# Hybrid decoder trunk: new places for row maxima, gate tiles, scan norm and latent tiles

## The chip, the cores and the metric

One core of a Trainium2 chip runs the whole two-layer trunk in one launch. The metric is device microseconds of that launch. The engines are told by short names: PE multiplies matrices, DVE and ACT do the elementwise work, SP issues the loads of weights, POOL issues the other transfers.

## The reference, cut to what matters

```python
D_MODEL, SEQ, DEPTH = 2048, 512, 2
def hybrid_layer(x, ...):
    h = rms_norm(x, norm_g)
    u = h @ w_in
    c_q, c_kv, k_pe, g_mla, u_conv, g_conv, z, xbc, dt_raw = jnp.split(u, offs, axis=-1)
    o_mla = mla_mixer(c_q, c_kv, k_pe, ...) * jax.nn.silu(g_mla)      # 6 heads, latent q 512, latent kv 256
    o_conv = conformer_conv_mixer(u_conv, ...) * jax.nn.silu(g_conv)  # 31 taps, 512 channels
    o_ssd = ssd_mixer(z, xbc, dt_raw, ...)                            # 12 heads, norm of y * silu(z)
    y = jnp.concatenate([o_mla, o_conv, o_ssd], axis=-1) @ w_out
    return x + y
```

`mla_mixer` norms c_q and c_kv, projects them, norms each head's query and key, rotates part of them and does causal softmax attention. `ssd_mixer` multiplies the scan's result y by silu(z) and norms it over its 768 channels.

## The kernel before, in words

All activations lie in SBUF with channels on partitions and the 512 positions along the free axis, 16 blocks of 128 channels. Every large product is done in three matmuls (L525 to L527): weights and activations are each split into a rounded part and the rest (`whi`, `wlo`; `hhi`, `hlo`), and the product of the two rests is left out.

**Units and tiles.** The input projection has 41 tiles of 128 output columns (`tiles_in`, L47): four cq, two ckv, one kpe, six gmla, eight of the convolution's input (ua and ug in turn), ten xbc, four gconv, six z. A tile is 16 blocks deep and is fed by two units of weights of 128x1024 (the first two tiles share four units, "first"). A unit takes PE 24 matmuls. For each, SP loads it into one of two `stage` buffers (L448), ACT copies it to one of three `whi` (L789) and DVE subtracts to make `wlo` (L1070). SP's load of a unit waits for the `wlo` of the unit two before. ACT's and DVE's share of unit u+3 is done at the beginning of step u, and ACT's waits until PE has used unit u.

**The order.** One list, `STEPS`, built by `steps` (L114) from the units and from `hooks` (L69), is walked by every engine. Step ("in", (j, half)) is half a tile, and the hooks at place 2j+half follow it. Each engine takes the list in order, so what waits on an engine holds back all that stands behind it there. On DVE a step first makes the `wlo` of unit u+3 and then, at half 1, takes the tile out of PSUM (`evac`, L1090). `acc_taken` counts those takings; PE waits for it before it begins a tile.

**Banks.** PSUM has eight banks: acc (2), S (2), T (2), M, O. Tiles alternate between the acc banks, but for tiles 2 and 3, which lie in S (`in_bank`, L314). Out rows use acc1, acc0, S0, T0 in turn.

**The latent tiles.** Hook "rx" (place 4) sums the squares of x on PE (`total`, L540: one fp32 matmul with ones into M); ACT turns it into 1/rms with an Ln and an Exp (`rsqrt`, L791, each with a table load). Then DVE and ACT run `latent` (L1186) for tiles 0 and 1 (evacuation, square, sum, split), and for tiles 2 to 5 at their own steps. Hook "cq_sum" (place 8) and "ckv_sum" (place 12) sum their squares on PE; for the latter ACT does Ln, Exp, Ln, Exp. Hooks "v" (places 13, 14) make the values in S and T, and ACT moves them out (L925). At the kpe tile ACT copies the rotated key half (`kr_both`), ahead of that.

**The attention.** For each of three pairs of heads: "proj", "head_sum" (sums of squares in S and T), ACT's Ln and Exp (`head_r`), "head_apply" for h=0 and h=1 (L1343: four DVE instructions each, the names `xg`, `key` for pair 2), "rotate". `row_max` and `row_rinv` (L1215) of score block n come at the beginning of step ("in", (14+n, 0)) on DVE; hook "scores" n is behind that step on PE and "turn_probs" n (transposes, L693) behind the next one.

**The end of a layer.** The scan's chunks (hooks "ssd_a", "ssd_b", places 54 to 72) write blocks 10 to 15 of `xg`; tile z i multiplies block 10+i by its gate and adds its square to `sqz` (three DVE instructions behind the gate, two for i=0). gconv i writes its gate to block 6+i, and "pw" f (places 78 to 81) multiplies the convolution's product into it. Step "turn" splits blocks 0 to 7 for the output projection. Step "ssd_sum" does the rest: blocks 8 and 9, ACT's Ln and Exp of the scan's sum (which PE makes in M within the second of the four "out2" units), then scaling and splitting of blocks 10 to 15. The out2 units hold output rows 0 and 1 in the order of `OUT2`:

```python
OUT2 = [(0, k) for k in range(10)] + [(1, k) for k in range(10)]
OUT2 += [(f, k) for f in range(2) for k in range(10, KX)]
```

## Time and profile before

| | |
|---|---|
| median of 3 runs | 1549.59 us (1548.27 to 1551.21) |
| the profiled execution | 1550.43 us |
| its span | 1548.6 us |
| PE busy | 1529.6 us, 99% |
| DVE busy | 1007.4 us, 65% |
| ACT busy | 687.2 us, 44% |
| mean granted clock | 0.999 |

A busy PE matmul of 512 columns is listed with 0.39 us, while back to back such matmuls start 0.23 us apart: the listed end of one overlaps the next. The stages of layer 0, by PE: start and first units to 37 us, latent tiles to 85, values to 110, projections to 216, attention beside tiles 14 to 26 to 430, scan beside the later tiles to 540, tail of the tiles to 601, output rows to 779. Layer 1 repeats them.

### The profile page before, as it was taken

To read this page: it belongs to the slowest core of one execution; us is meant where nothing else is said; L and a number is where in the kernel's file an instruction comes from. 1 tells how busy PE (TensorE), PEld (TensorE's weight loads), DVE (VectorE), ACT (ScalarE), POOL (GpSimd) and SP (SyncE) were. 2 spreads that over 40 slices of the span, in tenths; PEclk is the share of its full clock that TensorE was granted. 3 is DMA by queue.
4 is the path that set the end of the run, shared out by engine and by line. 5 is a ranking of instruction groups with operands and counts; after the bars stand their busy time and mean duration, and the time that the engine had idled before them with its cause. 6 is when DMAs were issued, how large, how long until landed. Compare 5 with 4: busy or idle time off the path is not lost.

```text
span 1548.6 us, 18424 instructions
## 1 busy us (share of the span) xinstructions
PE 1529.6 (99%) x7086; PEld 1225.9 (79%) x7086; DVE 1007.4 (65%) x1497; ACT 687.2 (44%) x1015; POOL 43.6 (3%) x84
## 2 busy tenths in 40 slices
PE   9999999999999999999999999999999999999999
PEld 7777777778888787788887777778778888878887
DVE  7544674989998777443455456658899978673221
ACT  7455543434456645211153555533444565552111
POOL 0000000000000000110000000000000000001010
PEclk9999999999999999999999999999999999999999
DMA  6322222222233223544432222222223333235442
GB/s 226 98 89 82 86 86 75 71 80 68 82 110 116 88 83 99 165 139 154 143 107 78 82 87 91 82 69 82 69 69 103 97 118 105 69 95 170 143 149 82
DMA packets 44839, 158.13 MB, mean 102 GB/s; under 512 B 5552, under 2 KB 5840, under 8 KB 44752
## 3 DMA queue, kind: packets, MB, share of 16 engines
q1 hardware_dynamic: 38448, 134.36, 26.8%
q0 software_dynamic: 6304, 22.60, 5.2%
q8 instruction: 56, 0.92, 0.2%
q14 instruction: 31, 0.25, 0.0%
HBM read 148.50 MB, written 8.44 MB: 101 GB/s over the span
## 4 chain that ended last, share of the span: by engine, by line
PE 82%; DVE 10%; ACT 5%; issue 2%; DMA 1%; SPq 0%; DVEq 0%; ACTq 0%
PE acc L525 18%; PE acc L527 18%; PE acc L526 18%; PE S L530 5%; PE S L525 3%; PE S L527 3%; PE S L526 3%; PE T L527 3%; PE T L526 3%; PE T L525 3%; DVE wlo L1070 2%; ACT L777 1%; PE M L530 1%; PE O L530 1%; DVE hlo L1173 1%
## 5 line engine op out<-in xcount | busy, mean ns | idle before, releaser
L525 PE MATMUL acc<-hhi,whi 128*128 128x512 f32 (+1 forms) x1504 | 599.9, 399 | 6.4 <-DVE wlo L1070 3.2
L527 PE MATMUL acc<-hhi,wlo 128*128 128x512 f32 (+1 forms) x1504 | 587.1, 390 | 0.0
L526 PE MATMUL acc<-hlo,whi 128*128 128x512 f32 (+1 forms) x1504 | 586.5, 390 | 0.0
L1070 DVE TENSOR_TENSOR wlo<-stage,whi 128x1024 fp32r<-128x1024 f32 (+2 forms) x251 | 299.5, 1196 | 409.2 <-ACT whi L789 405.8
L789 ACT ACTIVATE whi<-stage 128x1024 fp32r<-128x1024 f32 (+2 forms) x251 | 259.1, 1036 | 501.8 <-PE acc L527 282.8
L525 PEld LDWEIGHTS acc<-hhi,whi 128*128 128x128 f32 (+1 forms) x1504 | 281.5, 187 | 72.9 <-DVE wlo L1070 4.9
L527 PEld LDWEIGHTS acc<-hhi,wlo 128*128 128x128 f32 (+1 forms) x1504 | 281.3, 187 | 61.9
L526 PEld LDWEIGHTS acc<-hlo,whi 128*128 128x128 f32 (+1 forms) x1504 | 281.7, 187 | 60.3 <-issue 2.9
L1125 DVE SCALAR_TENSOR_TENSOR cacc<-glu,pv,cacc 128x512 f32<-128x512 f32 x240 | 168.8, 747 | 4.0
L777 ACT ACT_TABLE_LOAD x67 | 86.0, 1283 | 3.0 <-DVE small L1061 1.1
L525 PE MATMUL S<-hhi,whi 128*128 128x512 f32 x192 | 75.2, 392 | 0.1
L526 PE MATMUL S<-hlo,whi 128*128 128x512 f32 x192 | 74.7, 389 | 0.0
L527 PE MATMUL S<-hhi,wlo 128*128 128x512 f32 x192 | 74.7, 389 | 0.0
L525 PE MATMUL T<-hhi,whi 128*128 128x512 f32 x128 | 49.8, 389 | 0.0
L526 PE MATMUL T<-hlo,whi 128*128 128x512 f32 x128 | 49.8, 389 | 0.0
L527 PE MATMUL T<-hhi,wlo 128*128 128x512 f32 x128 | 49.8, 389 | 0.0
L1061 DVE SCALAR_TENSOR_TENSOR xb<-raw,pv,xb 128x512 f32<-128x512 f32 x60 | 45.0, 751 | 2.4
L777 ACT ACTIVATE prob<-S,cols 128x128 f32<-128x128 f32 (+3 forms) x48 | 25.4, 529 | 44.8 <-DVE cols L1222 38.4
L525 PEld LDWEIGHTS S<-hhi,whi 128*128 128x128 f32 x192 | 36.0, 188 | 8.6 <-DVE wlo L1070 1.0
L526 PEld LDWEIGHTS S<-hlo,whi 128*128 128x128 f32 x192 | 36.0, 188 | 7.7 <-issue 0.2
L527 PEld LDWEIGHTS S<-hhi,wlo 128*128 128x128 f32 x192 | 36.0, 188 | 7.5
L891 ACT ACTIVATE xb<-raw,pv 128x512 f32<-128x512 f32 x20 | 16.4, 819 | 46.5 <-DVE raw L1052 46.5
(239 smaller groups left out, 1566.2 us busy)
## 6 DMA issues: line engine op xcount, KB each, us to landing
stage<-weights SPq DMA_DIRECT2D x235, 512.0 KB, 3.4
y_features<-xg POOLq DMA_DIRECT2D x30, 256.0 KB, 4.2
acsb<-acs_rows POOLq DMA_DIRECT2D x16, 384.0 KB, 4.1
xr<-x_features POOLq DMA_DIRECT2D x16, 256.0 KB, 4.1
xr<-y_features POOLq DMA_DIRECT2D x16, 256.0 KB, 4.0
...
```

The lines of the kernel that those rows point to most:

```text
L525: nc.tensor.matmul(out, a, c, start=start, stop=False)
L526: nc.tensor.matmul(out, a, d, start=False, stop=False)
L527: return nc.tensor.matmul(out, b, c, start=False, stop=stop)
L530: return nc.tensor.matmul(out, a, b, start=start, stop=stop)
L777: nc.scalar.activation(out, in_, func, **more).then_inc(signal.sem, 1)
L789: nc.scalar.activation(whi[u % RING][:, 0:w], stage[u % STAGE][:, 0:w], ACT.Copy).then_inc(hi_done.sem, 1)
L891: nc.scalar.activation(xb[i // 5][:, i % 5, :], raw[:, 3:3 + SEQ], ACT.Identity, scale=par("scw", SSD_K * ch + 3), bias=par("scb", ch)).th ...
L1061: d(signal, nc.vector.scalar_tensor_tensor(out=out, in0=x, scalar=s, in1=y, op0=op0, op1=op1), go)
L1070: nc.vector.tensor_tensor(wlo[u % RING][:, 0:w], stage[u % STAGE][:, 0:w], whi[u % RING][:, 0:w].bitcast(F32), ALU.subtract).then_inc(lo_d ...
L1125: ins = nc.vector.scalar_tensor_tensor(out=cacc[:, j, :], in0=src, scalar=wt, in1=cacc[:, j, :], op0=ALU.mult, op1=ALU.add)
L1173: nc.vector.tensor_tensor(hlo[:, k, :], xg[:, k, :], hhi[:, k, :].bitcast(F32), ALU.subtract).then_inc(h_lo.sem, 1)
```

## The change

1. Tiles 0 to 5 use six banks (acc, S, T). PE's waits follow: tiles 6 and 7 wait for tiles 0 and 1, in layer 1 tiles 2 and 4 wait for the last output rows. "rx" goes from place 4 to 6 and then takes latent tiles 0 to 2; "cq_sum" goes from 8 to 10.
2. ACT's four operations at "ckv_sum" become Ln, Ln, Exp, Exp; its copy for `kr_both` goes from the kpe tile to "kd_turn".
3. The last pair's `head_apply` does both queries and the first key at once; `row_max(0)`, the second key and `row_rinv(0)` come at the beginning of step ("in", (13, 1)), ahead of that step's weights.
4. Tile order at the end: z0 to z2, gconv0, gconv1, z3 to z5, gconv2, gconv3.
5. The scan's sum is made on PE at place 79 (in T1) and its scaling on DVE at place 80, both ahead of the last tile. Step "turn_end" then splits blocks 10 to 15, 8, 9, and the output rows 0 and 1 take the blocks in that order.

```diff
-    t += [("gconv", j, [(_OFF["gconv"] + P * j, P)]) for j in range(4)]
-    t += [("z", j, [(_OFF["z"] + P * j, P)]) for j in range(6)]
-    return t
+    return t + z[0:3] + gate[0:2] + z[3:6] + gate[2:4]
...
-    put(4, "rx")
-    put(8, "cq_sum")
+    put(6, "rx")
+    put(10, "cq_sum")
...
+    put(79, "ssd_sum")
+    put(80, "ssd_scale")
...
+TURN_ORDER = list(range(8)) + list(range(10, KX)) + [8, 9]
+OUT2 = [(f, k) for f in range(2) for k in TURN_ORDER[:8]]
+OUT2 += [(f, k) for f in range(2) for k in TURN_ORDER[8:14]]
+OUT2 += [(f, k) for f in range(2) for k in TURN_ORDER[14:]]
...
-            return S[j - 2] if j in (2, 3) else acc[j % 2]
+            return (acc + S + T)[j] if j < 6 else acc[j % 2]
...
-                        if half == 0 and j >= 4:
-                            pe.wait_ge(acc_taken.sem, acc_taken.at(layer, j - 1))
+                        if half == 0 and j >= 6:
+                            pe.wait_ge(acc_taken.sem, acc_taken.at(layer, j - 5 if j < 8 else j - 1))
...
+                    elif name == "ssd_sum":
+                        pe.wait_ge(ssd_sq.sem, ssd_sq.at(layer, 1))
+                        pe.wait_ge(ssd_in.sem, ssd_in.at(layer, 8))
+                        total(ssd_sum, [sqz[:, :]], T[1])
                     elif name == "out2":
                         quarter, u = args[0], own[0]
                         if quarter < 2:
                             pe.wait_ge(acc_taken.sem, acc_taken.at(layer, len(TILES) - 1 + quarter))
-                        if quarter == 1:
-                            pe.wait_ge(ssd_sq.sem, ssd_sq.at(layer, 1))
-                            pe.wait_ge(pw_taken.sem, pw_taken.at(layer, 4))
-                            total(ssd_sum, [sqz[:, :]], M)
...
-                        rsqrt(None, rkc, O[:, 0:4], KV_LORA, 0)
-                        rsqrt(lat_r, rckv[:, :], M[:, :], KV_LORA, 0)
+                        a(None, rkc, O[:, 0:4], ACT.Ln, scale=1.0 / KV_LORA, bias=eps_col[:, 0:1])
+                        a(None, rckv[:, :], M[:, :], ACT.Ln, scale=1.0 / KV_LORA, bias=eps_col[:, 0:1])
+                        a(None, rkc, rkc, ACT.Exp, scale=-0.5)
+                        a(lat_r, rckv[:, :], rckv[:, :], ACT.Exp, scale=-0.5)
                     elif name == "kd_turn":
+                        act.wait_ge(kr_half.sem, kr_half.at(layer, 1))
+                        a(kr_both, kr2[64:128, :], kr2[0:64, :], ACT.Copy)
...
                 for name, args, own in STEPS:
-                    row_step = args[0] - SCORES_FROM if name == "in" and args[1] == 0 else -1
-                    if 0 <= row_step < 12:
+                    if name == "in" and args == (SCORES_FROM - 1, 1):
+                        row_max(0)
+                        apply_key(2, 1)
+                        row_rinv(0)
+                    row_step = args[0] - SCORES_FROM if name == "in" and args[1] == 0 else 0
+                    if 0 < row_step < 12:
                         row_max(row_step)
                     for u in own:
                         split(u + RING)
...
-                    elif name == "ssd_sum":
-                        split_branch(8, 10)
+                        split_branch(TURN_ORDER[:8], 0)
+                    elif name == "ssd_scale":
                         dve.wait_ge(ssd_r.sem, ssd_r.at(layer, 1))
                         for k in range(10, KX):
                             stt(branch_ready, xg[:, k, :], xg[:, k, :], par("sng", k - 10), rcq[:, :], ALU.mult,
                                 ALU.mult, go=k < KX - 1)
-                            if k >= 12:
-                                split_branch(k - 2, k - 1)
-                        split_branch(KX - 2, KX)
+                    elif name == "turn_end":
+                        split_branch(TURN_ORDER[8:], 8)
```

DVE at the first score block, before (`S` and `cols` are the row maxima's, `xg` and `key` the last pair's heads, `wlo` the weights' rests):

```order
L1070 TENSOR_TENSOR wlo_60<-stage_53,whi_57 128x1024
L1292 MEMSET glu 128x30
L1061 SCALAR_TENSOR_TENSOR glu<-acc,rx 128x512
L1061 SCALAR_TENSOR_TENSOR xg<-xg,pv,sqh 128x512
L1061 SCALAR_TENSOR_TENSOR xg<-xg,pv,sqh 64x512
L1061 SCALAR_TENSOR_TENSOR key_80<-key_80,pv,sqh 128x512
L1052 TENSOR_TENSOR key_80<-kr_91,sqh 64x512
L1052 TENSOR_TENSOR S<-S,const 128x128
L1222 TENSOR_REDUCE cols<-S 128x1
L1052 TENSOR_TENSOR S<-S,const 128x128
L1222 TENSOR_REDUCE cols<-S 128x1
L1070 TENSOR_TENSOR wlo_58<-stage_54,whi_55 128x1024
```

and with the change:

```order
L1067 SCALAR_TENSOR_TENSOR xg<-xg,pv,sqh 128x512
L1067 SCALAR_TENSOR_TENSOR xg<-xg,pv,sqh 64x512
L1067 SCALAR_TENSOR_TENSOR key_80<-key_80,pv,sqh 128x512
L1058 TENSOR_TENSOR key_80<-kr_91,sqh 64x512
L1058 TENSOR_TENSOR S<-S,const 128x128
L1228 TENSOR_REDUCE cols<-S 128x1
L1058 TENSOR_TENSOR S<-S,const 128x128
L1228 TENSOR_REDUCE cols<-S 128x1
L1067 SCALAR_TENSOR_TENSOR key_80<-key_80,pv,sqh 128x512
L1058 TENSOR_TENSOR key_80<-kr_91,sqh 64x512
L1235 RECIPROCAL cols<-cols 128x1 x2
L1076 TENSOR_TENSOR wlo_60<-stage_53,whi_57 128x1024
```

The two masked maxima stand ahead of the second key, and the weights' rest and the evacuation of tile 13 (`glu<-acc`) behind all of it.

ACT between the latent sums and the values, before (`cols` and `rckv` are the roots, `kr` the key half):

```order
L777 ACT_TABLE_LOAD
L777 ACTIVATE cols<-O,eps_col 128x4
L777 ACT_TABLE_LOAD
L777 ACTIVATE cols<-cols 128x4
L777 ACT_TABLE_LOAD
L777 ACTIVATE rckv<-M,eps_col 128x512
L777 ACT_TABLE_LOAD
L777 ACTIVATE rckv<-rckv 128x512
L789 ACTIVATE whi_56<-stage_53 128x768
L777 ACTIVATE kr_91<-kr_91 64x512
L789 ACTIVATE whi_57<-stage_54 128x1024
L925 ACTIVATE value<-S,cols 128x384 x2
```

and with the change:

```order
L781 ACT_TABLE_LOAD
L781 ACTIVATE cols<-O,eps_col 128x4
L781 ACTIVATE rckv<-M,eps_col 128x512
L781 ACT_TABLE_LOAD
L781 ACTIVATE cols<-cols 128x4
L781 ACTIVATE rckv<-rckv 128x512
L793 ACTIVATE whi_56<-stage_53 128x768
L793 ACTIVATE whi_57<-stage_54 128x1024
L930 ACTIVATE value<-S,cols 128x384 x2
L930 ACTIVATE value<-T,cols 128x384 x2
```

Two table loads are gone, and the copy of the key half no longer stands ahead of the values.

DVE from the turn on, before (after the eight splits of blocks 0 to 7):

```order
L1070 TENSOR_TENSOR wlo_59<-stage_53,whi_56 128x1024
L1052 TENSOR_TENSOR xg<-O,xg 128x512
L1070 TENSOR_TENSOR wlo_60<-stage_54,whi_57 128x1024
L1052 TENSOR_TENSOR temp<-acc,rx 128x512
L1052 TENSOR_TENSOR xg<-xg,temp_69 128x512
L1052 TENSOR_TENSOR temp<-xg 128x512
L1052 TENSOR_TENSOR kr_91<-kr_91,temp 128x512
L1070 TENSOR_TENSOR wlo_58<-stage_53,whi_55 128x1024
L1052 TENSOR_TENSOR xg<-M,xg 128x512
L1173 TENSOR_TENSOR hlo<-xg,hhi 128x512 x2
L1061 SCALAR_TENSOR_TENSOR xg<-xg,pv,rcq 128x512 x3
```

and with the change, from those eight splits on:

```order
L1179 TENSOR_TENSOR hlo<-xg,hhi 128x512 x8
L1076 TENSOR_TENSOR wlo_59<-stage_53,whi_56 128x1024
L1058 TENSOR_TENSOR xg<-O,xg 128x512
L1067 SCALAR_TENSOR_TENSOR xg<-xg,pv,rcq 128x512 x6
L1076 TENSOR_TENSOR wlo_60<-stage_54,whi_57 128x1024
L1058 TENSOR_TENSOR temp<-acc,rx 128x512
L1076 TENSOR_TENSOR wlo_58<-stage_53,whi_55 128x1024
L1058 TENSOR_TENSOR xg<-M,xg 128x512
L1179 TENSOR_TENSOR hlo<-xg,hhi 128x512 x8
```

The six scalings by `rcq` stand ahead of the last tile's evacuation (`temp<-acc`), and all eight remaining splits follow in one piece.

## Rows read from the trace of the kernel before

**Rows 1.** PE's waits over the whole span: engine, line, releaser, us in total, times, longest us.

```profile
PE acc L525 <- DVE wlo L1070: 3.2, 4, 1.4
PE T L693 <- ACT prob L777: 3.2, 2, 1.6
PE S L525 <- ACT value L925: 2.3, 2, 1.1
```

**Rows 2.** Timeline of PE: start us, us, engine line, out<-in, shape, count, [idle before <-releaser].

```profile
38.66 0.50 PE L525 MATMUL S<-hhi,whi 128*128 128x512 f32 x1
...
60.33 0.39 PE L527 MATMUL acc<-hhi,wlo 128*128 128x512 f32 x1
62.15 1.10 PE L530 MATMUL M<-sqh,ones 128*128 128x512 f32 x2 [1.43 <-DVE sqh L1052]
```

**Rows 3.** Timeline of DVE at the sum of squares' end in layer 0.

```profile
37.38 2.36 DVE L1070 TENSOR_TENSOR wlo<-stage,whi 128x1024 fp32r<-128x1024 f32 x2
```

**Rows 4.** Timeline of PE in layer 1 at the sum of the input's squares.

```profile
806.61 1.02 PE L530 MATMUL M<-sqh,ones 128*128 128x512 f32 x2
...
807.70 0.40 PE L526 MATMUL S<-hlo,whi 128*128 128x512 f32 x1
```

**Rows 5.** Timeline of ACT in layer 1 behind that sum.

```profile
807.94 1.28 ACT L777 ACT_TABLE_LOAD   x1
```

**Rows 6.** Timeline of DVE in layer 1, the first two latent tiles and a weight unit.

```profile
811.96 0.69 DVE L1052 TENSOR_TENSOR temp<-acc,rx 128x512 f32<-128x512 f32 x1 [2.78 <-ACT rx L777]
...
814.36 0.69 DVE L1052 TENSOR_TENSOR temp<-acc,rx 128x512 f32<-128x512 f32 x1
...
817.32 1.23 DVE L1070 TENSOR_TENSOR wlo<-stage,whi 128x1024 fp32r<-128x1024 f32 x1
```

**Rows 7.** Timeline of ACT ahead of the value rows.

```profile
100.73 0.63 ACT L777 ACTIVATE kr<-kr 64x512 f32<-64x512 f32 x1 [6.60 <-DVE kr L1052]
```

**Rows 8.** Timeline of PE around the first transposed probabilities, layer 0.

```profile
237.20 0.76 PE L693 MATMUL T<-const,prob 128*128 128x128 f32 x2 [1.59 <-ACT prob L777]
237.73 0.47 PE L525 MATMUL acc<-hhi,whi 128*128 128x512 f32 x1
...
240.16 0.63 PE L526 MATMUL acc<-hlo,whi 128*128 128x512 f32 x1
240.59 0.63 PE L527 MATMUL acc<-hhi,wlo 128*128 128x512 f32 x1
```

**Rows 9.** Stretch: us, PE busy (count), PEld, DVE, ACT, POOL, PEclk, DMA share, GB/s.

```profile
236.00:242.00 6.00, 4.69 (x14) 3.61 (x15) 3.29 (x6) 2.94 (x6) 0.00 (x0) 0.72 0.41 109
```

**Rows 10.** Timeline of DVE before those transposes.

```profile
226.23 1.40 DVE L1061 SCALAR_TENSOR_TENSOR xg<-xg,pv,sqh 128x512 f32<-128x512 f32 x2 [3.66 <-ACT sqh L777]
...
234.03 0.30 DVE L1052 TENSOR_TENSOR S<-S,const 128x128 f32<-128x128 f32 x1
```

**Rows 11.** Timeline of DVE at the weights behind a gate tile.

```profile
497.47 1.23 DVE L1070 TENSOR_TENSOR wlo<-stage,whi 128x1024 fp32r<-128x1024 f32 x1 [2.23 <-ACT whi L789]
```

**Rows 12.** Timeline of PE at the end of the tiles and in the first output rows.

```profile
593.15 0.40 PE L525 MATMUL acc<-hhi,whi 128*128 128x512 f32 x1
...
598.62 0.40 PE L525 MATMUL M<-pwhi,whi 128*128 128x512 f32 x1
...
607.42 1.10 PE L530 MATMUL M<-kr,ones 128*128 128x512 f32 x2 [0.35 <-DVE xg L1052]
608.85 0.50 PE L525 MATMUL acc<-hhi,whi 128*128 128x512 f32 x1 [0.33 <-DVE hlo L1173]
...
621.49 0.50 PE L525 MATMUL acc<-hhi,whi 128*128 128x512 f32 x1 [1.37 <-DVE wlo L1070]
```

**Rows 13.** Timeline of DVE from the turn to the scan's scaling.

```profile
594.01 4.90 DVE L1173 TENSOR_TENSOR hlo<-xg,hhi 128x512 fp32r<-128x512 f32 x8 [1.98 <-ACT hhi L807]
...
599.97 0.68 DVE L1052 TENSOR_TENSOR xg<-O,xg 128x512 f32<-128x512 f32 x1
...
612.50 2.08 DVE L1061 SCALAR_TENSOR_TENSOR xg<-xg,pv,rcq 128x512 f32<-128x512 f32 x3 [3.10 <-ACT rcq L777]
```

More of the change, by code:

```diff
@@ L57, in tiles_in @@
             t += [("xbc", 5 * g + i, [(_OFF["xbc"] + P * c, P)])]
-    t += [("gconv", j, [(_OFF["gconv"] + P * j, P)]) for j in range(4)]
-    t += [("z", j, [(_OFF["z"] + P * j, P)]) for j in range(6)]
-    return t
+    gate = [("gconv", j, [(_OFF["gconv"] + P * j, P)]) for j in range(4)]
+    z = [("z", j, [(_OFF["z"] + P * j, P)]) for j in range(6)]
+    return t + z[0:3] + gate[0:2] + z[3:6] + gate[2:4]
 TILES = tiles_in()
@@ L144, in steps @@
     return s, units
-OUT2 = [(0, k) for k in range(10)] + [(1, k) for k in range(10)]
-OUT2 += [(f, k) for f in range(2) for k in range(10, KX)]
+TURN_ORDER = list(range(8)) + list(range(10, KX)) + [8, 9]
+OUT2 = [(f, k) for f in range(2) for k in TURN_ORDER[:8]]
+OUT2 += [(f, k) for f in range(2) for k in TURN_ORDER[8:14]]
+OUT2 += [(f, k) for f in range(2) for k in TURN_ORDER[14:]]
 STEPS, UNITS = steps()
@@ L568, in _ @@
                         u, m = own[0], tile_columns(j)
-                        if half == 0 and j >= 4:
-                            pe.wait_ge(acc_taken.sem, acc_taken.at(layer, j - 1))
-                        if half == 0 and j == 2 and layer:
-                            pe.wait_ge(acc_taken.sem, acc_taken.at(layer - 1, len(TILES) + KX - 1))
+                        if half == 0 and j >= 6:
+                            pe.wait_ge(acc_taken.sem, acc_taken.at(layer, j - 5 if j < 8 else j - 1))
+                        if half == 0 and j in (2, 4) and layer:
+                            pe.wait_ge(acc_taken.sem, acc_taken.at(layer - 1, len(TILES) + KX - 2 + j // 2))
                         for k8 in range(8):
@@ L874, in _ @@
                         kind, i, _ = TILES[args[0]]
-                        if kind in ("cq", "ckv") and args[0] >= 2:
+                        if kind in ("cq", "ckv") and args[0] >= 3:
                             latent_hi(args[0])
-                        if kind == "kpe":
-                            act.wait_ge(kr_half.sem, kr_half.at(layer, 1))
-                            a(kr_both, kr2[64:128, :], kr2[0:64, :], ACT.Copy)
                         if kind == "ug":
@@ L898, in _ @@
                         rsqrt(rx_ready, rx[:, :], M[:, :], D_MODEL, 0)
-                        for j in range(2):
+                        for j in range(3):
                             latent_hi(j)
@@ L1015, in _ @@
                     elif name == "ssd_sum":
+                        act.wait_ge(ssd_sum.sem, ssd_sum.at(layer, 1))
+                        rsqrt(ssd_r, rcq[:, :], T[1][:, :], SSD_WIDTH, 0)
+                    elif name == "turn_end":
                         act.wait_ge(unit_used.sem, unit_used.at(layer, TILE_UNIT[len(TILES) - 1] + 1))
-                        act.wait_ge(pw_taken.sem, pw_taken.at(layer, 4))
-                        for k in range(8, KX):
-                            if k == 10:
-                                act.wait_ge(ssd_sum.sem, ssd_sum.at(layer, 1))
-                                rsqrt(ssd_r, rcq[:, :], M[:, :], SSD_WIDTH, 0)
+                        for k in TURN_ORDER[8:]:
                             if k >= 10:
                                 act.wait_ge(branch_ready.sem, branch_ready.at(layer, k - 9))
+                            else:
+                                act.wait_ge(pw_taken.sem, pw_taken.at(layer, k - 5))
                             branch_hi(k)
@@ L1167, in _, with split_branch @@
                                 x_add(3 * (k // 8) + i)
-                def split_branch(first, end):
-                    for k in range(first, end):
-                        dve.wait_ge(h_hi.sem, h_hi.at(layer, KX + k + 1))
+                def split_branch(ks, before):
+                    for i, k in enumerate(ks):
+                        dve.wait_ge(h_hi.sem, h_hi.at(layer, KX + before + i + 1))
                         nc.vector.tensor_tensor(hlo[:, k, :], xg[:, k, :], hhi[:, k, :].bitcast(F32),
@@ L1229, in row_rinv, with apply_query, apply_key @@
                         d(rinv_ready, nc.vector.reciprocal(rinv[h], rsum[h]))
[L1231 to L1233 removed]
+                def apply_query(p, h):
+                    q, r = QK[p], slice(64 * h, 64 * h + 64)
+                    stt(None, q[h], q[h], par("qn"), sqh[:, h, :], ALU.mult, ALU.mult, go=True)
+                    stt(None, q[2][r], q[2][r], par("qr")[r], sqh[r, h, :], ALU.mult, ALU.mult)
+                def apply_key(p, h):
+                    q, r = QK[p], slice(64 * h, 64 * h + 64)
+                    stt(None, q[3 + h], q[3 + h], par("kn"), sqh[:, 2 + h, :], ALU.mult, ALU.mult, go=True)
+                    tt(None, q[5][r], kr2[r, :], sqh[r, 2 + h, :], ALU.mult)
+                for name, args, own in STEPS:
+                    if name == "in" and args == (SCORES_FROM - 1, 1):
[4 more added lines that the diff above has]
+                    if 0 < row_step < 12:
                         row_max(row_step)
@@ L1260, in _ @@
                         kind, i, _ = TILES[j]
-                        if kind in ("cq", "ckv"):
+                        if kind in ("cq", "ckv") and j >= 3:
                             latent(j)
@@ L1464, in _ @@
                     elif name == "rx":
-                        for j in range(2):
+                        for j in range(3):
                             latent(j)
                     elif name == "turn":
-                        split_branch(0, 8)
-                    elif name == "ssd_sum":
-                        split_branch(8, 10)
+                        split_branch(TURN_ORDER[:8], 0)
+                    elif name == "ssd_scale":
                         dve.wait_ge(ssd_r.sem, ssd_r.at(layer, 1))
```

22 lines of the change are left out of this document (12 added, 10 removed).

## The prediction

> **What bounds the kernel now.** PE is listed busy for 99% of the span, and the change takes no matmul away and adds none, so only the time can go in which PE stands still. I first read PE's waits over the whole span [rows 1]: a handful, in the same places in both layers. Then PE's timeline at each of them gives its size. A unit of 24 matmuls takes 598.62 - 593.15 = 5.47 us, 0.23 us a matmul [rows 12], while a row lists 0.39; so a stall is the idle time shown plus 0.16. Check: the matmul at 60.33 should be followed at 60.56, the next work begins at 62.15, 1.59 late, and 1.43 + 0.16 is the same [rows 2]. So per layer: values 2.3 / 2 + 0.16, about 1.3 [rows 1]; first transposes 1.59 + 0.16 = 1.75 [rows 8]; output rows 0.35, 0.33 and 1.37, each + 0.16, together 2.53 [rows 12]. Layer 0 alone has the 1.59 at the cq sum. One thing more: behind the stall at 237.20 matmuls start 240.59 - 240.16 = 0.43 us apart and not 0.23 [rows 8]: the granted clock fell to 1.2 GHz of 2.4 after 1.75 us of standing still. Its mean over 236 to 242 is 0.72 [rows 9], which makes 0.28 x 6 = 1.7 us of work not done. The same stall in layer 1 did not bring that: the mean clock of the whole execution is 0.999, which is this one stretch (1.7 / 1548.6).
>
> **The sum, part by part.**
>
> *Six banks, later latent tiles.* The sum of the input's squares costs PE 807.70 - 806.61 - 0.23 = 0.86 us [rows 4]. In layer 0 it costs nothing now: PE may go on with tile 2 only at 38.66, since the unit's `wlo` ends at about 38.6, behind DVE's adding of squares [rows 2, 3]. Moved two units on, it leaves that wait uncovered and is paid in full: +0.86. In return the cq sum comes two units later. Its wait of 1.59 goes if all is in time. Take PE's begin of the square sum as zero. ACT finishes a `whi` at +1.3 and the roots at +5.3 (807.94 and 811.96 less 806.61) [rows 4 to 6]. The first latent tile takes 814.36 - 811.96 = 2.40, each further one 817.32 - 814.36 = 2.96, so three end at +13.7 and the `wlo` behind them at +14.9 [rows 6]. PE needs it after the sum and three units, at 0.86 + 3 x 5.47 = +17.3: 2.4 us to spare. Tile 3 is squared 2.1 us after that `wlo` (the 2.96 less its split of 0.8), at +17, and the cq sum needs it at +22.7. Tiles 4 and 5 no longer wait for a bank. So nothing else is late: 0.86 - 1.59 = -0.73, layer 0 only.
>
> Here a rule has to be weighed. A table load is listed with 1.28, and from the first load's start to the end of both roots there are 4.0 us (two loads, 0.7 and 0.6) [rows 5, 6]: nothing is added to a load. The Trainium skill ("ScalarE: Activation LUTs", What ACT_TABLE_LOAD costs) says that every switch of set costs about 2.66 us, load and drain together. By that, the roots would come at +8.1 and the `wlo` at +17.7, 0.4 late in each layer, and the sum below would be 0.8 smaller. The rows decide: I take 1.28.
>
> *Values.* The second value unit waits for ACT's first values, and those stand behind the copy of the key half, for which ACT idles 6.60 us until 100.73 [rows 7]. The copy moves behind the values, to where its 0.63 us stands between a gate and the dt chain, which PE meets two units later. Two loads fewer (2.6 us) start the rest earlier. First value tiles can then leave some 4 us earlier than now, against a stall of 1.3: all of it goes, in both layers. The first matmul after a stall also takes longer to the next, 0.1 us; with the stalls below four per layer, I take -0.2 a layer for that.
>
> *First row maxima.* DVE begins the last pair's heads at 226.23 and the maxima at 234.03, 7.8 us later [rows 10]. In between lie two heads of four instructions of 0.7 (two take 1.40), a `wlo` of 1.2 and an evacuation of 0.7. With the change six of the eight head instructions come first: 226.23 + 4.3 = 230.5. PE's scores are there one unit before its 235.45 (below), at 230.0. Four instructions of 0.3 end at 231.8, the second key at 233.2, the reciprocals at 233.6, ACT's scaling of the first head at 234.0, and PE is free at 237.20 - 1.75 = 235.45. Margin 1.4 us, so 1.75 goes, and so does what the second head's transposes wait between themselves: the two take 237.73 - 237.20 = 0.53 now and should take 0.22 [rows 8]. -2.06 in each layer. Behind the maxima on DVE's queue stand the `wlo` of PE's next unit (ready at 234.8, needed at 235.7) and the evacuation of tile 13, done at 235.6, which PE needs only after its transposes at 235.7. That one is near, and I leave it at nothing. With the stall the slow stretch should go, 1.7 us, once.
>
> *z tiles ahead.* Each brings two or three DVE instructions of 0.7, at most 2.15 us, before the next `wlo`. At those places DVE idles 2.23 and more in front of that `wlo`, waiting for ACT and so for PE [rows 11]. Cost nothing. Without that cover it would be up to 2.15 a tile, but the weights are three units ahead, and only a delay of more than a unit would reach PE.
>
> *The scan's norm ahead of the turn.* PE's sum costs the same 0.86 in its new place. There it follows z5's tile by two units and two pointwise products of 12 matmuls (2.8 each), some 16 us, so its input is ready. Behind it PE has a unit and the third product, 8.2 us, until the turn; ACT needs about 1.3 for a `whi`, as above, and 4.0 for the roots, and has them 3 us before the turn. Now the turn itself; zero is the end of that product, 593.3, some 0.86 later in the new order. The eight splits end at +5.6, the `wlo` and the product's gate at +7.4 (599.97 + 0.68) [rows 13]. Six scalings at 2.08 / 3 = 0.69 end at +11.5, the next `wlo` at +12.7, the evacuation of tile 40 at +13.3. PE needs the latter for output row 1, after a unit, the last product (2.8) and the first out2 unit: 2 x 5.47 + 2.8 - 0.16 = +13.6. Margin 0.3 us, the tightest of the change. From there: gate, `wlo` and product to +17, eight splits at 0.6 to +21.9, the first of them at +17.7 for a need at +19.0, and each next one needed 0.68 later. The next `wlo` comes at +23.1 for +24.5. So all three stalls go: -2.53 a layer. If splits and scalings had stayed behind the sum, as now, nothing would. The last two of the four waits for `wlo` in rows 1, (3.2 - 2 x 1.37) / 2 = 0.23 each, stand behind the first pointwise product, and they stay: nothing ahead of them changes.
>
> Sum: layer 0: -0.73 - 1.3 - 2.06 - 1.7 - 2.53 - 0.2 = -8.5; layer 1: -1.3 - 2.06 - 2.53 - 0.2 = -6.1; together -14.6. From the profiled execution's 1550.43: **1535.8 us**. That execution is 0.84 above the median of the runs shown, which may well be its one stretch of half clock; runs without it would go from some 1548.8 to the same 1535.8.
>
> **The rivals.** *B, the half clock comes all the same.* PE still stands still for 1.1 us at 37.5 and at the start; one such stretch costs 1.7: 1537.5. For it: it came once in two equal stalls. Against: no other stall brought it.
>
> *C, a cover fails in part.* The margins of 0.3 us (tile 40's evacuation) and 0.1 (tile 13's) are no larger than what two equal stretches differ by, and three latent tiles in a row are a new burst. Should the maxima still be late by what they are now, 4.1 come back and perhaps the 1.7: 1541.6; half of it, 1538.8.
>
> *D, the stalls only move.* Each time PE comes sooner, it waits as long at the next thing. Then only the slow stretch goes, 1550.43 - 1.7 = 1548.7. Against: every chain that I followed starts from PE's own progress (a bank done, a unit used), so it moves with PE.
>
> *E, slower: the turn's chain stands bare.* DVE now does six scalings (4.1), the last `wlo` (1.2) and the evacuation (0.7) between the pointwise product and output row 1, and they wait for ACT's 4.0 us of roots. If those roots came only after the turn's splits, all 10 us would stand before PE in each layer: 1535.8 + 20 = 1556. It decides where DVE reaches the scaling more than 7 us later than reckoned; then the change loses. Against: the roots are reckoned 3 us ahead of the turn and over 10 us ahead of the scaling.
>
> **How the numbers follow.** As reckoned (1535.0 to 1537.0): 0.60. B: 0.14. C: 0.14. More goes than reckoned (another 0.4 to 0.8 of small waits; under 1534.6): 0.05. D: 0.04. E: 0.03. The forecast is the first. The range runs from 1534.4 to 1540.5, over B and most of C, and leaves out D, E and C's far end. About 0.2%, 3.1 us, is what a measurement of this kernel can tell from no change: faster 0.93 (all but D and E), same 0.04, slower 0.03.
>
> **What would show it.** In the changed kernel's waits of PE: no wait for `prob` at L693's new line, none for `value`, none ahead of the sum over `kr`, and none of 1.4 for `wlo` in the out rows; 0.23 for the pointwise product still there; a wait of about 1 us for `wlo` at 37.5. The clock at 2.4 GHz from the start to the end. DVE's evacuation of tile 40 ends just before PE's first matmul of output row 1. It would be wrong if a new wait on `acc` evacuation or `wlo` of over 0.5 us appears, at tile 13, behind the three latent tiles, or in output row 1.

## The result and the profile after

The changed kernel takes 1534.78 us in the median (1534.68 to 1534.90, 4 runs) beside 1549.07 us (1548.27 to 1551.21, 4 runs) for the kernel before: a ratio of 0.9905, with a 95% interval of 0.9893 to 0.9917. The profiled execution took 1534.9 us with a span of 1533.1, against 1550.43 and 1548.6: 15.5 us less. The forecast was 1535.8, with a range from 1534.4 to 1540.5: the measured time lies inside it, and 0.2 below the case that was given 0.60 (1535.0 to 1537.0).

The page of the changed kernel, from its parts on busy time and on the chain:

```profile
span 1533.1 us, 18419 instructions
...
PE 1524.4 (99%) x7086; PEld 1225.4 (80%) x7086; DVE 1007.6 (66%) x1497; ACT 683.0 (45%) x1013; POOL 43.5 (3%) x84
...
PE 92%; DVE 5%; ACT 1%; issue 1%; DMA 0%; SPq 0%; DVEq 0%; ACTq 0%
```

The same work is done; ACT is busy for 4.2 us less, with 65 table loads and not 67. Each layer saves two loads at the ckv sum and has one more behind the scan's roots, which now stand amid the gate tiles (loads at 580.69, 582.69 and 594.30, where the kernel before has two, at 608.53 and 610.54). The waits of PE in the changed kernel, over the whole span, answer to [rows 1]:

```profile
PE acc L529 <- DVE wlo L1161: 1.1, 1, 1.1
PE M L534 <- DVE eps_col L1038: 1.1, 1, 1.1
PE acc L529 <- DVE hlo L1144: 1.1, 2, 0.8
PE S L529 <- DVE wlo L1076: 1.0, 1, 1.0
PE acc L529 <- DVE wlo L1076: 0.4, 2, 0.2
PE S L534 <- DVE sqh L1058: 0.3, 1, 0.3
```

The waits for `prob` (3.2) and `value` (2.3) are gone, and so are the two of 1.4 for `wlo` in the output rows. L1161, L1144 and `eps_col` belong to the start. What is left is the uncovered 1.0 that the forecast had for layer 0, 0.2 a layer behind the first pointwise product, and one wait of 0.3 that the kernel before has too (945.22 there). PE's timeline shows the uncovered wait at its place, against [rows 2], and then the sum of squares (an fp32 matmul is listed as two):

```profile
37.63 0.50 PE L529 MATMUL S<-hhi,whi 128*128 128x512 f32 x1 [1.03 <-DVE wlo L1076]
...
48.64 1.02 PE L534 MATMUL M<-sqh,ones 128*128 128x512 f32 x2
```

DVE of the changed kernel around the first row maxima, which answers to [rows 10]:

```profile
226.09 0.75 DVE L1067 SCALAR_TENSOR_TENSOR key<-key,pv,sqh 128x512 f32<-128x512 f32 x1
226.76 0.68 DVE L1058 TENSOR_TENSOR key<-kr,sqh 64x512 f32<-64x512 f32 x1
227.47 0.30 DVE L1058 TENSOR_TENSOR S<-S,const 128x128 f32<-128x128 f32 x1
...
230.29 0.36 DVE L1235 RECIPROCAL cols<-cols 128x1 f32<-128x1 f32 x2
230.69 1.22 DVE L1076 TENSOR_TENSOR wlo<-stage,whi 128x1024 fp32r<-128x1024 f32 x1
231.87 0.08 DVE L1314 MEMSET glu<- 128x30 f32 x1
231.98 0.69 DVE L1067 SCALAR_TENSOR_TENSOR glu<-acc,rx 128x512 f32<-128x512 f32 x1
```

and PE behind it, against [rows 8]:

```profile
232.31 0.38 PE L697 MATMUL T<-const,prob 128*128 128x128 f32 x2
232.82 0.47 PE L529 MATMUL acc<-hhi,whi 128*128 128x512 f32 x1
```

Both transposes run without a wait, but the next tile starts at 232.82, 0.15 behind the end of tile 13's evacuation (231.98 + 0.69 = 232.67). That start is 0.29 later than 232.31 + 0.22 = 232.53, where PE would have been free: a new small wait. The windows of 8 us from 234 on, before and after (us, then busy times by engine, then PEclk, the granted clock), against [rows 9]:

```profile
234.00:242.00 8.00, 6.30 (x22) 4.59 (x21) 5.12 (x10) 3.86 (x10) 0.00 (x0) 0.79 0.30 82
```

```profile
234.00:242.00 8.00, 8.00 (x39) 6.23 (x39) 4.26 (x8) 3.88 (x8) 0.00 (x0) 1.00 0.53 168
```

The clock stays at 2.4 GHz. At the turn, DVE of the changed kernel, against [rows 13]:

```profile
588.35 4.91 DVE L1179 TENSOR_TENSOR hlo<-xg,hhi 128x512 fp32r<-128x512 f32 x8 [1.96 <-ACT hhi L811]
593.17 1.22 DVE L1076 TENSOR_TENSOR wlo<-stage,whi 128x1024 fp32r<-128x1024 f32 x1
594.30 0.69 DVE L1058 TENSOR_TENSOR xg<-O,xg 128x512 f32<-128x512 f32 x1
595.02 4.07 DVE L1067 SCALAR_TENSOR_TENSOR xg<-xg,pv,rcq 128x512 f32<-128x512 f32 x6
599.12 1.23 DVE L1076 TENSOR_TENSOR wlo<-stage,whi 128x1024 fp32r<-128x1024 f32 x1
600.27 0.68 DVE L1058 TENSOR_TENSOR temp<-acc,rx 128x512 f32<-128x512 f32 x1
```

and PE's first matmul of output row 1:

```profile
601.24 0.39 PE L529 MATMUL acc<-hhi,whi 128*128 128x512 f32 x1
```

The evacuation of tile 40 ends at 600.95, 0.29 ahead of PE; the forecast said 0.3.

**Where the 15.5 us came from.** PE's starts of the same matmuls in both traces (for the last matmul, its end), and how much more the changed kernel is ahead at each:

| up to | before | after | ahead by | of it here |
|---|---|---|---|---|
| third group of the first unit (start) | 11.95 | 10.91 | 1.04 | 1.04 |
| ckv sum of layer 0 | 84.89 | 83.13 | 1.76 | 0.72 |
| transposes of `kd` | 112.80 | 109.67 | 3.13 | 1.37 |
| first product of probabilities and values | 246.48 | 239.95 | 6.53 | 3.40 |
| last product `pw` | 598.62 | 592.96 | 5.66 | -0.87 |
| ckv sum of layer 1 | 851.98 | 842.45 | 9.53 | 3.87 |
| transposes of `kd` | 879.88 | 868.99 | 10.89 | 1.36 |
| first product of probabilities and values | 1012.28 | 999.69 | 12.59 | 1.70 |
| last `pw` | 1364.42 | 1352.69 | 11.73 | -0.86 |
| end of the last matmul | 1545.35 | 1529.77 | 15.58 | 3.85 |

The 0.86 is the scan's sum, now ahead of `pw` 3 and no longer in the output rows; the turn is worth 3.0 net in each layer. A full 1.0 us lies in the first 12 us, where nothing was changed:

```profile
11.95 0.50 PE L525 MATMUL acc<-hhi,whi 128*128 128x512 f32 x1 [1.76 <-DVE hlo L1138]
```

```profile
10.91 0.50 PE L529 MATMUL acc<-hhi,whi 128*128 128x512 f32 x1 [0.81 <-DVE hlo L1144]
```

Ahead of the first of these ACT had waited 1.75 us for a load of weights and began the second `whi` at 9.11; in the changed kernel it began it at 8.13, 0.98 earlier.

### The profile page after: what moved, and what is told of

Read it like the earlier page. It is cut to its first block, busy times and chain, and to the rows that moved or that the text cites. A ratio compares the mean times of both kernels' runs of the same rounds, so it can differ in the third digit from the quotient of the medians.

```text
span 1533.1 us, 18419 instructions
## 1 busy us (share of the span) xinstructions
PE 1524.4 (99%) x7086; PEld 1225.4 (80%) x7086; DVE 1007.6 (66%) x1497; ACT 683.0 (45%) x1013; POOL 43.5 (3%) x84
## 4 chain that ended last, share of the span: by engine, by line
PE 92%; DVE 5%; ACT 1%; issue 1%; DMA 0%; SPq 0%; DVEq 0%; ACTq 0%
PE acc L529 20%; PE acc L531 19%; PE acc L530 19%; PE S L534 5%; PE S L529 4%; PE S L530 4%; PE S L531 4%; PE T L531 4%; PE T L530 4%; PE T L529 4%; PE M L534 1%; PE O L534 1%; DVE wlo L1076 1%; PE T L534 1%; PE T L697 1%
## 5 line engine op out<-in xcount | busy, mean ns | idle before, releaser
L529 PE MATMUL acc<-hhi,whi 128*128 128x512 f32 (+1 forms) x1440 | 573.8, 398 | 2.9 <-DVE wlo L1161 1.1
L531 PE MATMUL acc<-hhi,wlo 128*128 128x512 f32 (+1 forms) x1440 | 561.7, 390 | 0.0
L530 PE MATMUL acc<-hlo,whi 128*128 128x512 f32 (+1 forms) x1440 | 560.8, 389 | 0.0
L531 PEld LDWEIGHTS acc<-hhi,wlo 128*128 128x128 f32 (+1 forms) x1440 | 268.9, 187 | 59.3
L529 PE MATMUL T<-hhi,whi 128*128 128x512 f32 x192 | 75.5, 393 | 0.0
L531 PE MATMUL T<-hhi,wlo 128*128 128x512 f32 x192 | 74.7, 389 | 0.0
L530 PE MATMUL T<-hlo,whi 128*128 128x512 f32 x192 | 74.7, 389 | 0.0
L529 PEld LDWEIGHTS T<-hhi,whi 128*128 128x128 f32 x192 | 36.0, 188 | 7.9 <-issue 0.5
L530 PEld LDWEIGHTS T<-hlo,whi 128*128 128x128 f32 x192 | 36.0, 188 | 7.9 <-issue 0.5
L531 PEld LDWEIGHTS T<-hhi,wlo 128*128 128x128 f32 x192 | 36.0, 188 | 7.5
```

Source lines behind the costliest of these rows:

```text
L529: nc.tensor.matmul(out, a, c, start=start, stop=False)
L530: nc.tensor.matmul(out, a, d, start=False, stop=False)
L531: return nc.tensor.matmul(out, b, c, start=False, stop=stop)
```

## Experiments

The theory is the forecast's: each stall stands alone, so each part can be undone alone and gives back its own term. The main rival: the parts cover one another. Five kernels undo one part of the change or half of one, and two do one part alone. Where not said otherwise five or four runs were timed.

### The row maxima back

```diff
-                    if name == "in" and args == (SCORES_FROM - 1, 1):
-                        row_max(0)
-                        apply_key(2, 1)
-                        row_rinv(0)
-                    row_step = args[0] - SCORES_FROM if name == "in" and args[1] == 0 else 0
+                    row_step = args[0] - SCORES_FROM if name == "in" and args[1] == 0 else -1
...
```

with `head_apply` for h=0 and h=1 as before.

> The changed kernel (1534.8) with the order of the last pair's heads and of the first row maxima as before. Theory, every stall stands alone: PE waits for the first probabilities again, 1.75 us in each layer, and the small wait of 0.3 behind tile 13's evacuation is covered by it, so about +3.5 us: 1538.3, clock 2.4 GHz throughout or, if the long stall brings the half clock, up to 1540.0 with a stretch of 1.2 GHz right behind it in layer 0. Rival, the parts cover one another (the earlier values already bring the scores forward): under +1, 1535.8 at most.

Measured: 1540.1 us (1538.09 to 1540.46, 5 runs). Its waits hold the old one again, and the window from 234 on, beside the same stretch of layer 1 (997 to 1003), shows the clock:

```profile
PE T L697 <- ACT prob L781: 3.4, 2, 1.7
```

```profile
234.00:240.00 6.00, 5.50 (x17) 4.29 (x18) 2.56 (x4) 2.88 (x6) 0.00 (x0) 0.72 0.54 168
...
997.00:1003.00 6.00, 5.31 (x24) 4.26 (x24) 2.72 (x5) 2.94 (x6) 0.00 (x0) 1.00 0.50 169
```

PE stands still for 1.86 us ahead of 234.40 and for 1.88 ahead of 997.59 (1.70 and 1.72 idle + 0.16). Behind the first the clock falls, with a mean of 0.72 as in [rows 9]; behind the second it doesn't. Four of the five runs lie at 1540.1 to 1540.5, with a mean granted clock of 0.999 on record; the one at 1538.09 has 1.000. So the stalls alone give the 1538.3 of the theory, and a stretch of half clock on top of them the 1540. The rival (under 1536) is out.

### The scan's norm back at the turn

```diff
-    put(79, "ssd_sum")
-    put(80, "ssd_scale")
...
+                        if quarter == 1:
+                            pe.wait_ge(ssd_sq.sem, ssd_sq.at(layer, 1))
+                            pe.wait_ge(pw_taken.sem, pw_taken.at(layer, 4))
+                            total(ssd_sum, [sqz[:, :]], M)
```

with the old `OUT2`, scaling and splits; the tile order stays new.

> The changed kernel with the scan's sum, roots, scaling and the order of the splits at the turn as before; the order of the last ten tiles stays new. Theory: the three stalls of output rows come back (0.51, 0.50 and 1.54 of standing still, and a slow second matmul behind each), +3.0 us a layer, 1540.8. Rival, the new tile order already puts the sum's squares earlier and takes part of the waits: 1536 to 1538.

Measured: 1539.32 us (1539.16 to 1539.79), 2.2 a layer and not 3.0. PE's timeline around the sum:

```profile
600.31 0.39 PE L527 MATMUL acc<-hhi,wlo 128*128 128x512 f32 x1
600.54 1.09 PE L530 MATMUL M<-kr,ones 128*128 128x512 f32 x2
601.96 0.50 PE L525 MATMUL acc<-hhi,whi 128*128 128x512 f32 x1 [0.33 <-DVE hlo L1174]
```

The sum starts 0.23 behind the matmul ahead of it: the first of the three stalls of [rows 12] isn't there. In layer 1 most of the second is gone too: the next matmul starts 1.10 behind the sum's start (1362.74 and 1363.84), against 1.42 above. The time lies between the theory's 1540.8 and the rival's 1538, and the rival is right in part: the new tile order took these waits, as the next run shows.

### The tile order alone

The kernel before with the new `tiles_in` and nothing else.

> The kernel before with the new order of the last ten tiles and nothing else. Theory, DVE's two or three more instructions behind a z tile stand in its idle time: no difference from the kernel before (ratio 1.000). Rival, a wlo comes late behind them: up to +2 us a layer. Rival, the earlier squares shorten the waits of the output rows: -1 to -2 us.

Measured: 1546.53 us (1545.74 to 1548.49, 11 runs), ratio 0.9983 (0.9974 to 0.9992). The last rival holds. In DVE's timeline the gate of the last pointwise product ends before PE's sum, which starts at 605.82, has to wait:

```profile
603.64 1.23 DVE L1070 TENSOR_TENSOR wlo<-stage,whi 128x1024 fp32r<-128x1024 f32 x1 [2.22 <-ACT whi L789]
604.79 0.69 DVE L1052 TENSOR_TENSOR xg<-M,xg 128x512 f32<-128x512 f32 x1
```

In the kernel before the three instructions of z5 (2.15 us) stood ahead of that `wlo`, which started at 605.45, and the gate ended at 607.27. With gconv3 last they are not there. The wait of 0.33 behind the sum is smaller as well, 0.21 in layer 0. Between the last `pw` and the ckv sum of the next layer the trace is 0.69 shorter (851.98 - 598.62 = 253.36 before, 850.20 - 597.53 = 252.67 here), and from the last `pw` of layer 1 to the end 0.78: 1.5 in all. The medians differ by 2.65 (1549.18 for the kernel before); 13 of its 19 runs have a mean clock under 1.000, against 4 of 11 here. Compared at the same recorded clock they differ by 1.8 (1547.90 and 1546.11 at 1.000, six and seven runs) and by 1.3 (1549.27 and 1547.93 at 0.999).

### The values: the copy, or the loads

```diff
                         if kind == "kpe":
+                            act.wait_ge(kr_half.sem, kr_half.at(layer, 1))
+                            a(kr_both, kr2[64:128, :], kr2[0:64, :], ACT.Copy)
```

> The changed kernel with ACT's copy of the rotated key at the kpe tile again, ahead of the values; the roots stay in the order Ln, Ln, Exp, Exp. Theory, the copy was what the values stood behind: the second value unit waits about 1.3 us in each layer again, +2.7: 1537.5. Rival, the two saved table loads did it: 0 to +0.3, 1535.1 at most.

and, the other way round, the copy late and the roots apart:

```diff
-                        a(None, rkc, O[:, 0:4], ACT.Ln, scale=1.0 / KV_LORA, bias=eps_col[:, 0:1])
...
+                        rsqrt(None, rkc, O[:, 0:4], KV_LORA, 0)
+                        rsqrt(lat_r, rckv[:, :], M[:, :], KV_LORA, 0)
```

> The changed kernel with the roots of the ckv sum in the order Ln, Exp, Ln, Exp (two table loads more in each layer, 2.6 us of ACT); the key's copy stays late. Theory, the copy was the cause and the loads only cost time that ACT has: 0, 1534.8. Rival, the loads were the cause: +1 to +2.7, up to 1537.5.

Measured: 1535.71 us (1535.5 to 1535.85) with the copy back, 1535.14 (1535.04 to 1535.3) with the roots apart. ACT's and PE's timelines of the kernel with the copy back:

```profile
97.88 0.63 ACT L781 ACTIVATE kr<-kr 64x512 f32<-64x512 f32 x1 [6.60 <-DVE kr L1059]
98.54 1.06 ACT L793 ACTIVATE whi<-stage 128x1024 fp32r<-128x1024 f32 x1
99.51 1.03 ACT L931 ACTIVATE value<-S,cols 128x384 f32<-128x384 f32 x2
```

```profile
100.21 0.41 PE L529 MATMUL S<-whi,ckvhi 128*128 128x384 f32 x1 [0.26 <-ACT value L931]
```

The values still stand behind the copy, as in [rows 7], but counted from the ckv sum (82.91 here, 84.89 before) the copy comes at +15.0 and not at +15.8. The loads cost ACT 2.6 us, of which 0.9 reaches DVE's work on the key, since ACT then idles for 1.72 until PE frees the buffer of its next `whi`. So the stall shrinks to 0.26 + 0.16 = 0.42, twice 0.42 = 0.84 in all, and 1535.71 is 0.8 to 0.9 above the changed kernel (1534.91 in the runs below, 1534.78 above). That is neither the theory's 1537.5 nor the rival's 1535.1 at most: each had one cause do all. With the roots apart there is no wait for `value`, and the first value leaves 12.63 us behind the ckv sum, the same as in the changed kernel (83.27 and 83.13 are the sums):

```profile
95.90 1.03 ACT L928 ACTIVATE value<-S,cols 128x384 f32<-128x384 f32 x2
```

```profile
95.76 1.03 ACT L930 ACTIVATE value<-S,cols 128x384 f32<-128x384 f32 x2
```

Moving the copy takes the whole stall of 1.3; the two loads saved, with the copy in its old place, take 0.9 of it. They are not additive.

### The latent tiles back

```diff
-    put(6, "rx")
-    put(10, "cq_sum")
+    put(4, "rx")
+    put(8, "cq_sum")
...
-            return (acc + S + T)[j] if j < 6 else acc[j % 2]
+            return S[j - 2] if j in (2, 3) else acc[j % 2]
```

> The changed kernel with two banks for tiles 0 and 1 and S for 2 and 3, and the sums of squares at places 4 and 8 again. Theory: the wait of 1.59 at the cq sum of layer 0 returns and the wait of 1.0 for the third unit's rest hides behind the sum again; net +0.7, layer 0 only: 1535.5. Rival, the six banks also save in layer 1: +1.5 or more. Rival, they save nothing: 0.

> The same kernel as e3_latents_back, whose profiled execution was disturbed (4889 us). Theory: in layer 0 the cq sum waits 1.6 us again and the 1.0 at the third unit's rest goes, and layer 1 stays: a span 0.7 us longer than the changed kernel's, 1535.5. The timed runs of e3_latents_back (1535.6 to 1536.1) say that it may be 1.2; then the trace should show a second wait.

Measured: 1535.64 to 1536.09 us in three timed runs (the profiled execution, at 4891 us, is left out), and the second time 1535.57 us (1534.81 to 1535.67), beside the changed kernel run again:

> The changed kernel, unaltered, beside the three others: 1534.8, within 0.3 us.

Measured for the unaltered kernel: 1534.91 us (1534.73 to 1535.12). So +0.7, or up to 1.1 by the first. The second trace puts it at 0.93: from the third group of matmuls to the ckv sum it takes 83.80 - 10.65 = 73.15, the changed kernel 83.13 - 10.91 = 72.22, and behind that both take the same. That trace has the wait that the theory names, and no other that the changed kernel lacks:

```profile
PE M L534 <- DVE sqh L1058: 1.6, 1, 1.6
```

Behind it PE had stood still for 1.57 + 0.16 = 1.73 us, and the clock of the next 6 us is 2.4 GHz all the same:

```profile
61.00:67.00 6.00, 5.98 (x25) 4.62 (x26) 1.89 (x2) 4.29 (x5) 0.00 (x0) 1.00 0.24 73
```

### The maxima alone

The kernel before with the maxima's part of the change.

> The kernel before with the last pair's heads and the first row maxima moved and nothing else. Theory: 1.75 us less in each layer, and no stretch of half clock: against runs of the kernel before without such a stretch -3.5 us, against runs with it -5.2. Rival, without the earlier values and the rest the maxima are not earlier against PE: under 1 us.

Measured: 1544.36 us (nine runs from 1544.04 to 1544.96, one at 1548.35), ratio 0.9975 (0.9965 to 0.9984); the median is 4.8 less than that of the runs of before beside it (1549.18, 19 runs). Both numbers of the theory can be read off at the recorded clocks: against the six of these runs with a mean clock of 1.000 (median 1547.90) the nine runs gain 3.6, against those with 0.999 (1549.27) 5.0. In the trace the clock is 1.0, and it gains 3.37 us in layer 0 and 1.74 in layer 1 at this place (214.47 and 246.48 against 213.47 and 242.11; 981.88 and 1012.28 against 977.50 and 1006.16), as with the whole change. This part needs none of the others.

### How near tile 40's evacuation is

```diff
+                        tt(None, temp[:, :], rcq[:, :], rcq[:, :], ALU.mult)
+                        tt(None, temp[:, :], rcq[:, :], rcq[:, :], ALU.mult)
                     elif name == "turn_end":
```

> The changed kernel with two further DVE instructions of 0.7 us right behind the six scalings of the scan's blocks (their result is not used). It measures how near the evacuation of tile 40 is to output row 1. Theory: PE has 0.3 us to spare there, so 1.4 - 0.3 = 1.1 us appear as a wait ahead of output row 1 in each layer: +2.2, with the slow matmul behind a stall +2.4: 1537.2. Rival, the evacuation is not what binds and its time can be made up: 0.

Measured: 1537.07 us (1536.92 to 1537.26). DVE and PE:

```profile
599.11 1.42 DVE L1058 TENSOR_TENSOR temp<-rcq 128x512 f32<-128x512 f32 x2
600.57 1.23 DVE L1076 TENSOR_TENSOR wlo<-stage,whi 128x1024 fp32r<-128x1024 f32 x1
601.71 0.68 DVE L1058 TENSOR_TENSOR temp<-acc,rx 128x512 f32<-128x512 f32 x1
```

```profile
602.49 0.47 PE L529 MATMUL acc<-hhi,whi 128*128 128x512 f32 x1 [1.11 <-DVE wlo L1076]
```

The margin of 0.3 is real. The two instructions move what follows on DVE by 1.45 us (600.57 less 599.12), and 1.45 - 0.29 = 1.16 of that reaches PE; the time is 2.3 us longer, 1.15 a layer. The row names `wlo` as the releaser, but that `wlo` ended at 601.80; PE went on 0.10 behind the evacuation's end (602.39).

### Two steps further

In v3_key_and_squares the second key goes behind tile 13's evacuation, and in layer 0 the last four squares of x go one step later, behind the next `wlo`:

```diff
                         row_max(0)
-                        apply_key(2, 1)
                         row_rinv(0)
...
                             evac(j, glu[:, i, PADC:PADC + SEQ], half=True)
+                            if i == 0:
+                                apply_key(2, 1)
...
-                    if name == "first" and args == (1,) and layer == 0:
-                        for k in range(6, KX):
+                    if name == "first" and args in ((1,), (2,)) and layer == 0:
+                        for k in (range(6, 12) if args == (1,) else range(12, KX)):
                             x_add(k)
```

(the same on ACT). And v4_norm_of_conv_earlier is v3 with

```diff
-    put(75, "ln_apply", 0)
-    put(76, "ln_apply", 1)
+    put(74, "ln_apply", 0)
+    put(75, "ln_apply", 1)
```

> The changed kernel with two steps moved: the second key of the last pair behind tile 13's evacuation, and the last four squares of the input one step later in layer 0. Theory: the 0.3 us ahead of tile 15 go in each layer and the 1.2 at the third unit's rest in layer 0, together -1.8: 1533.0. Rival, the rest of the fourth unit is late in its place: -0.6 only, 1534.2.

> v3_key_and_squares with both halves of the convolution's norm one place earlier (74 and 75 for 75 and 76), where DVE idles 5 us. Theory: the wait of 0.4 behind the first pointwise product goes in each layer, -0.8 against v3: 1532.2. Rival, the norm now holds up the rest of a unit or the evacuation of tile 37: 0 or slower than v3 by up to 2 us a layer.

Measured: 1532.95 us (1532.62 to 1533.03) and 1531.6 (1531.23 to 1531.84). The first is 1.96 below the changed kernel, 1.8 was expected. In its trace the tile behind the first transposes starts 0.14 behind them (230.82 and 230.96) and not 0.51: with the second key out of the way the wait for tile 13's evacuation is gone. All the waits of PE that v4 has left:

```profile
PE acc L529 <- DVE hlo L1144: 1.3, 2, 1.1
PE M L534 <- DVE eps_col L1038: 1.1, 1, 1.1
PE acc L529 <- DVE wlo L1161: 0.9, 1, 0.9
```

They are those of the start. v4 beats the changed kernel by 3.3 us; against the kernel before it has the ratio 0.9885 (0.9869 to 0.9902). The move of v4 gave 1.35 and not 0.8. In the traces the tail of the tiles is shorter by 0.53 in layer 0 and 0.50 in layer 1, and the wait ahead of a head sum of layer 1, which v3 still has at 932.51, is gone, worth another 0.33. That wait is hardly the move's doing: the kernel with the two added instructions has none there either. What goes with it is how soon DVE's `wlo` begins behind the start of ACT's `whi`: 1.51 us in v3 (921.40 and 922.91) and 1.53 in the changed kernel, which wait, 1.16 in v4 (921.25 and 922.41) and 1.17 with the added instructions, which don't. What delays DVE by that third of a microsecond stays open.

## Why the prediction came out as it did

The mechanism was right: the forecast stalls went, each ended by the chain that was named. Three steps failed: the starting point, which was 1.0 us too high and makes the whole difference between 1535.8 and 1534.8, and two terms put at nothing, the evacuation of tile 13 (0.3 to 0.4 a layer) and what the z tiles leave behind (0.7 to 0.8 a layer alone). That the parts sum to 14.6 against 14.5 is partly luck. In each layer the maxima were put 0.36 too high and the scan's norm 0.47 too low, with 0.2 set aside for slow matmuls in between.

**The starting point was 1.0 us too high.** The sum was made from the profiled 1550.43, and its 0.84 above the median was said to be perhaps "its one stretch of half clock". Its third group of matmuls started at 11.95, behind 1.76 of idle time. In the changed kernel that is 10.91, in the kernel before with the tile order alone 11.00, with the maxima alone 10.97, and in the changed kernel run again 10.96. In the eight others that ran undisturbed it lies between 10.65 and 11.10. So the late start belonged to that execution, behind a load of weights that came late. Subtract it, and the 14.6 of the sum stand against 14.5. The timed runs agree: the prediction put runs without a slow stretch at 1548.8, and the eight runs of before with a recorded clock of 1.000 have a median of 1547.9.

**Latent tiles, -0.73: right,** 0.72, and 0.93 in the trace that undoes them, whose wait is 1.57 and not 1.43. The chain too: from PE's sum at 48.64 the `wlo` behind three latent tiles ends at 63.55, +14.9 as reckoned, and PE needs it at +17.3. The rule of the Trainium skill ("ScalarE: Activation LUTs", What ACT_TABLE_LOAD costs) would have had it at +17.7 with a wait in each layer; the trace has none, so its 2.66 us a switch isn't what this sequence pays, and the row's 1.28 is.

**Values, -1.3: right in size** (1.37 and 1.36). The first value leaves 4.8 us earlier behind the ckv sum (12.63 for 102.36 - 84.89 = 17.47), where "some 4 us" was said. But "two loads fewer (2.6 us) start the rest earlier" has no part in it: with the loads back it leaves as early. The copy's move suffices; the loads alone bring 0.9.

**First maxima, -2.06: right in mechanism, 0.3 too much.** What failed is "That one is near, and I leave it at nothing". The evacuation of tile 13 was reckoned 0.1 ahead of PE and ended 0.14 behind the moment PE was free. From DVE's first head instruction to that end it was reckoned 9.4 us and took 9.60 (223.07 to 232.67). The excess is in the head instructions, put at 0.7 each: six of them took 4.40 for 4.3, the second key 1.51 for 1.4, and the rest is 0.04 at the memset and the evacuation. PE then started the tile 0.29 late, and the matmul behind a stall adds its 0.1. Net 1.7 in layer 1, and 3.4 with the slow stretch in layer 0. With the second key behind the evacuation (v3) the wait is gone.

**Half clock, -1.7 once: right in that execution.** Rival B is out: in all ten traces without the 1.75 us stall at the first probabilities (the one of 4889 us aside) the clock reads 1.0, though each of them still stands still at the start for 1 us and more.

**z tiles at nothing: wrong.** The step named the work ahead of each `wlo` that the z tiles bring and found it covered, which it is. It didn't ask what leaves: z5's three instructions were in front of the last pointwise product's gate, for which PE's sum waited. Alone the order gains 0.7 to 0.8 a layer. In the whole change these are the first of the three stalls that the next step counts and part of the second, so the sum wasn't harmed.

**Scan's norm, -2.53: right,** 3.0 with the slow matmuls. I had set 0.2 a layer aside for the slow matmul behind each stall; the two of these stalls that end in a matmul of a weight unit add 0.1 each (before, 608.85 to 609.18 is 0.33 and not 0.23, 621.49 to 621.83 is 0.34), and PE's total took 0.93 there and 0.86 in the new place. That makes 2.8; the rest of the 3.0 lies in no single place. Rival C's place was real (0.29 of margin, shown by the two added instructions); of its two margins tile 40's held, and tile 13's of 0.1 didn't. Nor did E: the roots were never late.

## What to carry to other kernels

Where the busiest engine is at 99%, price each stall from the timeline (idle plus what the listed durations hide), follow the chain that ends it back to that engine's own progress, and then a sum by parts can hold: here each part was within 0.5 us, and the sum within 0.1 by errors that cancelled. Where a margin is a tenth, price every instruction ahead of it from its own row, and ask of each moved step what it no longer stands in front of, too. Before a sum is built on one profiled execution, compare its first microseconds with another's: a late start looks like part of the kernel. And compare the times of runs that have the same mean clock on record: it takes apart what a median mixes.

## What the runs showed of the chip

One stall brings the half clock and another of the same length doesn't. The stall of 1.74 to 1.88 us ahead of the first transposes is followed by a stretch with a mean granted clock of 0.72 over 6 us in layer 0, and by 1.00 in layer 1, in all three traces that have it (before, the tile order alone, maxima back). Inside the slow stretch matmuls start 0.43 us apart, which is the lower of the two levels, 1.2 GHz. The 1.73 at the cq sum is followed by 1.00, and so are those of 1.54 in the output rows.

The timed runs show it too, since each has its mean granted clock on record. For the 35 runs of the kernel before that have one:

| mean clock | runs | time, us | median |
|---|---|---|---|
| 1.000 | 8 | 1546.91 to 1548.44 | 1547.9 |
| 0.999 | 16 | 1548.97 to 1550.25 | 1549.4 |
| 0.998 | 7 | 1548.97 to 1551.87 | 1550.7 |
| 0.997 | 4 | 1550.83 to 1551.40 | 1551.1 |

One stretch of 6 us at 0.72 takes 1.7 us, 0.001 of the span. So, by an estimate from these rounded clocks, the kernel before has none of them in a quarter of its executions, one in about half, and about two in the rest (their medians are 2.8 and 3.2 above the first row's). The tile order alone (1545.74 to 1546.60 at 1.000, 1547.80 to 1548.49 at 0.999) and the maxima back (1538.09 against 1540.08 to 1540.46) split the same way. Of 52 timed runs of the kernels without the long stall 50 read 1.000, and their spread within a kernel is mostly 0.2 to 0.9 us. The exceptions are a run with the roots apart (0.999, 1535.30, no longer than the others) and the run of the maxima alone at 1548.35, which reads 0.949: that would be far more than its 4 us, and it is unexplained. The changed kernel against the runs of before at 1.000 is 1547.9 less 1534.8, 13.1 us, near the 12.9 us that the waits alone make; the other 1.2 of the medians' 14.3 is such stretches. What decides whether a stall brings the stretch stays open.
